# Gate tables by column blocks, early work in another order, and the first one-hots made on GpSimd, in a two-block transformer kernel

## The reference

```python
def block(xb):                                   # 128 tokens
    q = (xb @ w_query).reshape(TOKEN_BLOCK, P_HEADS, 2, P_HALF)
    s = jnp.einsum('thpk,hpnk->thpn', q, sub_keys).astype(jnp.float32)
    sv, si = lax.top_k(s, P_TOPK)                # 16 of 128 keys, twice
    cand = (sv[:, :, 0, :, None] + sv[:, :, 1, None, :]).reshape(TOKEN_BLOCK, P_HEADS, P_TOPK * P_TOPK)
    cidx = (si[:, :, 0, :, None] * N_KEYS + si[:, :, 1, None, :]).reshape(TOKEN_BLOCK, P_HEADS, P_TOPK * P_TOPK)
    fv, fpos = lax.top_k(cand, P_TOPK)
    eidx = jnp.take_along_axis(cidx, fpos, axis=-1)
    g = jax.nn.softmax(fv, axis=-1)
    u = u_tab[eidx]
    act = jax.nn.gelu(jnp.einsum('td,thkd->thk', xb, u).astype(jnp.float32), approximate=False)
    return jnp.einsum('thk,thkd->td', (g * act).astype(xb.dtype), v_tab[eidx])
```

## Time and profile before

| | us |
|---|---|
| median of 3 runs (2775.04 to 2776.07) | 2775.61 |
| the profiled execution | 2776.91 |
| its span | 2775.0 |
| first gate table, last gate table | 1548.7, 1827.7 |
| first dense values, last | 1850.6, 2761 |

### The profile page before, as it was taken

How to read it: one execution, slowest core, us unless ns; L and a number is a source line. 1 busy time by engine, 2 the same in 40 slices (tenths; PEclk the granted TensorE clock), 3 DMA queues, 4 the chain that set the end, 5 groups by cost and what they waited for, 6 DMA issues and landing times.

```text
span 2775.0 us, 24927 instructions
## 1 busy us (share of the span) xinstructions
PE 2532.4 (91%) x8876; PEld 1459.4 (53%) x8876; DVE 1487.6 (54%) x3441; ACT 652.0 (23%) x1559; POOL 314.1 (11%) x287
## 2 busy tenths in 40 slices
PE   6999999999999999998998877668999999989877
PEld 3454555444444444454586665445666666656533
DVE  5444454220033433236456878856777676766675
ACT  2022364010000012224233445421111112111120
POOL 0000000000000000000001001212222222222230
PEclk9999999999999999999999999889999999999989
DMA  9621021112156411110244656779999999999995
GB/s 368 236 92 61 31 71 51 61 61 91 60 227 227 151 61 61 67 55 31 94 172 148 242 187 229 306 265 354 405 387 388 388 389 400 395 400 379 369 370 208
DMA packets 120742, 592.33 MB, mean 213 GB/s; under 512 B 10000, under 2 KB 42768, under 8 KB 76592
## 3 DMA queue, kind: packets, MB, share of 16 engines
q0 software_dynamic: 40656, 321.93, 29.4%
q1 hardware_dynamic: 76944, 247.48, 24.4%
q10 hardware_dynamic: 3024, 21.40, 1.9%
HBM read 571.90 MB, written 18.87 MB: 213 GB/s over the span
## 4 chain that ended last, share of the span: by engine, by line
PE 73%; DMA 14%; DVE 10%; issue 1%; ACT 1%; SPq 1%; POOL 0%; DVEq 0%; ACTq 0%; POOLq 0%
PE PS L609 24%; PE PS L1579 12%; PE PS L1628 11%; DMA arena<-in_u_turned 9%; PE PS L639 8%; PE PS L1151 4%; PE PS L1197 3%; PE PS L794 2%; DMA arena<-in_peer_uv 1%; PE PS L1602 1%; PE PS L814 1%; PE PS L803 1%; DMA arena<-in_ada 1%; DVE arena L2221 1%; PE PS L1172 1%
## 5 line engine op out<-in xcount | busy, mean ns | idle before, releaser
L1579 PE MATMUL PS<-hT,arena 128*128 128x256 f32 x2048 | 488.4, 395 | 60.4 <-DMA arena<-in_u_turned 60.4
L1579 PEld LDWEIGHTS PS<-hT,arena 128*128 128x128 f32 x2048 | 406.5, 199 | 171.6 <-DMA arena<-in_u_turned 71.1
L609 PE MATMUL PS<-arena,ring 128*128 128x512 f32 x832 | 359.2, 593 | 2.1 <-issue 0.8
L609 PE MATMUL PS<-hT,ring 128*128 128x256 f32 (+1 forms) x928 | 303.2, 486 | 7.0 <-ACT arena L1779 4.1
L2342 POOL DMA_INDIRECT arena<-in_peer_uv,arena x151 | 176.2, 1167 | 1158.3 <-DVE arena L2153 465.7
L609 PEld LDWEIGHTS PS<-arena,ring 128*128 128x128 f32 x832 | 157.0, 190 | 203.2 <-issue 201.9
L609 PEld LDWEIGHTS PS<-hT,ring 128*128 128x128 f32 x928 | 179.4, 196 | 124.7 <-issue 103.5
L2182 DVE CUSTOM_DVE_ANT_0 arena<-arena 128x1024 f32<-128x1024 f32 x151 | 183.9, 1222 | 97.5 <-DMA arena<-in_peer_uv,arena 95.5
L639 PE MATMUL PS<-hT,ring 128*128 128x512 f32 x512 | 221.9, 596 | 1.7 <-ACT hT L429 1.7
L1628 PE MATMUL PS<-arena,hT 128*128 128x512 f32 x384 | 173.6, 598 | 14.1 <-DVE hT L2231 14.1
L2199 DVE SCALAR_TENSOR_TENSOR arena<-arena 128x1024 f32<-128x1024 f32 x114 | 146.1, 1281 | 42.8 <-ACT arena L1796 42.5
(11 more groups left out here) (349 smaller groups left out, 2893.6 us busy)
## 6 DMA issues: line engine op xcount, KB each, us to landing
ring<-in_wstream SPq DMA_DIRECT2D x45, 2048.0 KB, 7.9
arena<-in_u_turned SPq DMA_DIRECT2D x128, 512.0 KB, 9.0
arena<-in_peer_uv SPq DMA_DIRECT2D x128, 512.0 KB, 9.2
arena<-in_ada POOLq DMA_DIRECT2D x24, 2048.0 KB, 9.4
gate_tables<-arena ACTq DMA_DIRECT2D x16, 1024.0 KB, 5.8
arena<-gate_tables SPq DMA_DIRECT2D x16, 1024.0 KB, 22.7
arena<-in_peer_uv,arena POOLq DMA_INDIRECT x151, 9.4
xT<-in_xT POOLq DMA_DIRECT2D x1, 2048.0 KB, 18.6
```

The costliest lines, as they stand in the source:

```text
L609: ins = pe.matmul(o, l, r, start=(a == 0), stop=(a == len(lhs) - 1))
L1579: ins = pe.matmul(dense_bank(j), ubuf[j % 3][:, tile(k)], hT[:, k, 256:512], start=(k == 0), stop=(k == KD - 1))
```

## The change

Five things are changed at once.

1. **First one-hots on GpSimd.** They leave VectorE, are made in GpSimd's queue between gathers, and go to six buffers instead of two. An alternative way to make them on ScalarE, not used before, is deleted.
2. **Another row of beats.** 20 beats in place of 24, with one pick in each of the first 12, two in the next four, three in the last four: NEARLY is 32 in place of 56. Jobs of block 3 are mixed in from the third on. All tables lie in beats 12 to 19, eight in each, after the dots of their beat; before, four in each of beats 8 to 23. The dense dots ahead of the loop lie in beats 11 to 19 by the table `DOT_PAIRS`, the last three pairs behind the last tables. Beats 0 to 8 have their values between the queries.
3. **Gate tables in DRAM by column blocks.** The store now writes 512-byte pieces to 16 blocks, and the load of a block is one run of 8 KB for each partition. Before, the store was one run of 8 KB and the load was in 512-byte pieces.
4. **Gates of the dense blocks in one go.** Instead of an exponential, a reciprocal and a product for each head, one exponential over 128 columns for each block, and three VectorE operations (`dense_gates`).
5. **Numbers that follow:** 1.78 picks for a chunk, `turn(xT, 1)` at chunk 80 in place of 70, the first result store at chunk 100 in place of 80.

```diff
-NBEAT = 24
+NAONE = 6
+NBEAT = 20
 def first_pick(b):
-    return 2 * b if b < 16 else 32 + 3 * (b - 16)
+    return b if b < 12 else 12 + 2 * (b - 12) if b < 16 else 20 + 3 * (b - 16)
-GATHER_JOB_AT = {4: 1, 11: 2, 18: 3, 22: 4}
+BEAT_JOB = [(2, 0), (2, 1), (3, 0), (2, 2), (2, 3), (3, 1), (2, 4), (2, 5), (3, 2), (3, 3), (2, 6), (2, 7),
+            (3, 4), (3, 5), (3, 6), (3, 7)]
+GATHER_JOB_AT = {11: 1, 16: 2}
+def values_after(b):
+    return 10 + (5 * b + 1) // 2
+QBEAT = 9
+DOT_PAIRS = {11: 1, 12: 2, 13: 2, 14: 1, 15: 1, 16: 1, 17: 1, 19: 3}
+TABLE_BEAT = 12
+def beat_tables(b):
+    return range(8 * (b - TABLE_BEAT), 8 * (b - TABLE_BEAT) + 8) if b >= TABLE_BEAT else range(0)
 def pick_at(chunk):
-    return NEARLY + (max(0, chunk) * 173) // 100
+    return NEARLY + (max(0, chunk) * 178) // 100
...
             def load_gates(blk):
-                sp.dma_start(gstage[blk % 2].rearrange("p (a c) -> p a c", a=16),
-                             gates_in_dram[:, :, blk * P:(blk + 1) * P].rearrange("a p c -> p a c")).then_inc(g_loaded[blk % 2], 16)
+                sp.dma_start(gstage[blk % 2], gates_in_dram[blk]).then_inc(g_loaded[blk % 2], 16)
...
-            for b in range(6, NBEAT):
-                values(beat_picks(b - 1))
-                if b >= 7:
-                    for q in range(4):
...
-                        if b >= 8:
-                            gate_tables(4 * (b - 8) + q)
+            for b in range(QBEAT, NBEAT):
+                if b > QBEAT:
+                    values(beat_picks(b - 1))
+                if b < NBEAT - 1:
+                    beat_dots(b)
+                if b in (12, 16):
+                    turn_picks(b // 16)
+                for g in beat_tables(b):
+                    gate_tables(g)
+            beat_dots(NBEAT - 1)
             values(beat_picks(NBEAT - 1))
...
                 if g % 4 == 3:
                     act.wait_ge(g_ev, g + 1)
-                    act.dma_start(gates_in_dram[tg], gstage[tg % 2]).then_inc(g_stored[tg % 2], 16)
+                    act.dma_start(gates_in_dram[:, :, tg * P:(tg + 1) * P].rearrange("b p c -> p b c"),
+                                  gstage[tg % 2].rearrange("p (b c) -> p b c", b=16)).then_inc(g_stored[tg % 2], 16)
...
+            def dense_gates(td):
+                q = slice(NGT * PH + PH * td, NGT * PH + PH * td + PH)
+                g = gate[:, 2 + td, :].rearrange("p (h e) -> p h e", h=PH)
+                dve.wait_ge(gates_ex, td + 1)
+                own(dve.tensor_reduce(gsum[:, 0, q], g, AXX, ALU.add))
+                own(dve.reciprocal(gsum[:, 1, q], gsum[:, 0, q]))
+                dve.tensor_tensor(g, g, gsum[:, 1, q].unsqueeze(2).to_broadcast([P, PH, PK]), ALU.mult).then_inc(picks_ok, 1)
...
+            def first_one_hots(g):
+                if g % 32 == 0:
+                    pool.wait_ge(picks_ev, g // 32 + 1)
+                if g >= NAONE:
+                    pool.wait_ge(g_pe, g + 1 - NAONE)
+                pick_i, pick_g = picked[g // 32][0], picked[g // 32][2]
+                for q in range(4):
+                    c = 4 * (g % 32) + q
+                    ins = pool.tensor_scalar(aone[:, g % NAONE, q, :], const("iota"), pick_i[:, c:c + 1], pick_g[:, c:c + 1],
+                                            ALU.is_equal, ALU.mult)
+                ins.then_inc(a_ok, 1)
+
+            made = 0
             for n in range(NPICK):
                 t, e, j = n // NSLOT, n % NSLOT, slot_of(n)
+                while made < 64 and PREVIOUS[n] is not None and PREVIOUS[n] >= first_pick(TABLE_BEAT + made // 8):
+                    first_one_hots(made)
+                    made += 1
```

More of the change, by code:

```diff
@@ L107, in on_pe @@
     return n < NEARLY
-def made_on_dve(g):
-    return True
-MADE_DVE, MADE_ACT = [0], [0]
-for _g in range(64):
-    MADE_DVE.append(MADE_DVE[-1] + made_on_dve(_g))
-    MADE_ACT.append(MADE_ACT[-1] + (not made_on_dve(_g)))
-def dense_pair(b, q):
-    m = 3 * (b - 7) // 2 + q
-    return m + 1 if 7 <= b < 15 and m < 3 * (b - 6) // 2 else 0
 def pick_at(chunk):
-    return NEARLY + (max(0, chunk) * 173) // 100
+    return NEARLY + (max(0, chunk) * 178) // 100
 TURN, PE_BEFORE, DVE_BEFORE = [0] * NPICK, [0] * (NPICK + 1), [0] * (NPICK + 1)
@@ L322, in build @@
         over = cst[:, CCOL["mask"]:CCOL["iota"]]
-        pick_i, pick_j, pick_g, minus_i, minus_g = (over[:, tile(q)] for q in range(5))
-        away = over[:, 5 * P:9 * P].rearrange("p (q n) -> p q n", q=4)
+        picked = [[over[:, tile(3 * td + q)] for q in range(3)] for td in range(2)]
         g2row = sq
@@ L1569, in _ @@
                     ins.then_inc(g2_pe, 1)
-                if i >= 13 and i % 4 == 1:
-                    values(beat_picks((i - 9) // 4 - 1))
+                for b in query_beats(i):
+                    values(beat_picks(b))
             key_scores(15)
@@ L1860, in _ @@
                 if b in GATHER_JOB_AT:
-                    hd = GATHER_JOB_AT[b]
-                    gate_exps(JOB[hd // PH, hd % PH])
-                if b in (8, 16):
-                    copy_picks(b // 8 - 1)
-                if b >= 7:
-                    for q in range(4):
-                        if q < 2 and dense_pair(b, q):
-                            dense_gelu(dense_pair(b, q) - 1)
-                        if b >= 8:
-                            g = 4 * (b - 8) + q
-                            if not made_on_dve(g):
-                                first_one_hots(g)
-                            if g >= 1:
-                                copy_gate_table(g - 1)
-            copy_gate_table(63)
+                    gate_exps(GATHER_JOB_AT[b])
+                if b in (11, 15):
+                    dense_gate_exps(b // 15)
+                if b < NBEAT - 1:
+                    for m in range(DOT_PAIR0[b], DOT_PAIR0[b + 1]):
+                        dense_gelu(m)
+                if b in (12, 16):
+                    copy_picks(b // 16)
+                for g in beat_tables(b):
+                    copy_gate_table(g)
+            for m in range(DOT_PAIR0[NBEAT - 1], DOT_PAIR0[NBEAT]):
+                dense_gelu(m)
             m = AHEAD // 2
@@ L2262, in _ @@
             job(0)
-            gated = 0
             for b in range(NBEAT):
                 if b < 16:
-                    k = JOB[2 + b // 8, b % 8]
-                    job(k, gated)
-                    gated = k
-                picks = beat_picks(b)
-                dot(picks[0])
-                if b in (16, 19, 23):
-                    pick_gates(gated)
-                for n in picks[1:]:
+                    job(JOB[BEAT_JOB[b]])
+                if b == 0:
+                    pick_gates(0)
+                for n in beat_picks(b):
                     dot(n)
@@ L2300, in _ @@
                     hd = (n + back) // PK
-                    if (n + back) % PK == 0 and 5 <= hd < NGT * PH:
-                        piece(JOB[hd // PH, hd % PH])
+                    if (n + back) % PK == 0 and 3 <= hd < NGT * PH:
+                        piece(hd if piece is pick_gates else JOB[hd // PH, hd % PH])
                 if n >= NSLOT and n - NSLOT in LAST_AT:
```

145 lines of the change are left out of this document (55 added, 90 removed).

## The result

The changed kernel takes 2813.64 us (median of 4 runs, 2805.68 to 2818.76), the kernel before 2775.84 on the same chip (2775.04 to 2782.68). The ratio is 1.0128, with a 95% interval of 1.0097 to 1.0159: slower by 38 us, where 2722 was forecast and the range ended at 2800. The profiled execution took 2816.74 us, its span is 2814.7.

What follows compares the result with a forecast made beforehand. It took VectorE's queue to set the time before 1828 us and the DMA engines after 1851, TensorE close behind. Terms 0 - 83 + 5 + 9 + 16 = -53 from the median of 2775.6 gave 2722 us, range 2665 to 2800.

Steps and rivals of the forecast that it cites:

- t: Table stage: time of one 128x128 one-hot on GpSimd, taken as 0.5 us between ends of 0.27 and 0.93.
- rival A: Table stage: slow GpSimd one-hots, by the operation itself or standing still beside VectorE; 2800 at 0.8 us; chance 0.30.
- the formula: Table stage: sum of beats from values, dots, tables, gathers and 32 one-hots each; 196 us against 279, -83.
- Early part, 0: 1373 to 1549 us: VectorE has less to do, but TensorE's order of dots gives it back; 0.
- ScalarE behind the stores in pieces, +5: Table stage: copies and pick weights stand behind gate-table stores in 512 B pieces on ScalarE's queue; +5 us.
- rival D: Table stage: ScalarE stands behind the stores in pieces for 50 us, not 5; about 2767; chance 0.04, no change.
- Between the stages, +9: Last table to first dense values: three pairs of dots and u loads come ahead, 22.9 us becomes 32; +9.
- Dense loop, +16 in all: Dense loop: 24 more gathers cost time, partly given back by spare DMA share, shorter pauses and cheaper gate loads; +16 us.
- -15 for the pieces: Dense loop: 14 gate loads in 8 KB instead of 512 B pieces save between 4 and 25 us; -15 taken.
- +62 - 25 + 4 = +41: Dense loop: 24 added gathers +62, spare DMA share at the end used -25, last token block finished later +4.
- Rival C: Dense loop: held by late loads, not DMA time, added gathers in slack; gains about 50, 2656 us; chance 0.09.
- Rival B: Table stage: one-hots below 0.4 us, TensorE bounds most beats; about 2685 to 2700 us; chance 0.17.

Runs made afterwards that it cites:

- part 3 alone: The kernel before with only the gate tables in DRAM by column blocks (512-byte pieces in stores, 8 KB in loads); 2721.37 us, 0.9811.

## Why the prediction was wrong

**The step that failed is t, the time of a one-hot on GpSimd.** The prediction took 0.5 us, between VectorE's 0.27 and a gather's 0.93, since "128 columns of the same work are nearer to VectorE's row than to a gather". It is 0.782 alone and 0.94 with VectorE's two-input instructions beside it. So rival A came, with both of the causes that it named: the operation alone is 0.782 (72 us above 256 x 0.5), and the overlap with VectorE adds 41, where it was reckoned at 62. The two, 113 us, are as large as the whole difference between the stage forecast (196) and measured (308.5).

That the formula is so near at this t, 305 us at 0.93, is in part luck. It left out TensorE's low clock behind the waits: the values of this stage take 41.8 us where the same values take 30.3 with the one-hots on VectorE, and a beat's last eight table matmuls take 2.08 where eight take 1.05 at the full clock. By these rows that is an estimated 20 us, on the chain. It counted on the other side every gather of a beat, of which the chain shows one, and TensorE's 23 us in beat 13 fell under the longer one-hots.

The time shows the rest: by the prediction's own 26 us for each 0.1, a t of 0.94 gives some 2836. The measured 2813.64 is lower, mostly because the loop gained 3 us where it was to lose 16. The nearest row was chosen by kind of work and not by engine; the gather of 0.93, the one row of GpSimd's queue that was looked at, was the nearer one. Of the -83 forecast, +29.5 came.

The Trainium skill was weighed there. By its "GPSIMD Engine Reference", sections 3.1 and 4.1, I had estimated 0.28 us and a dispatch, with one-input work near line rate. The trace disagrees: 0.78 us at two operations and 0.59 at one, of which some 0.36 to 0.40 is fixed, against 0.27 on VectorE. Its "SBUF — State Buffer", section "Who interferes with whom", says that a VectorE instruction with two SBUF inputs contends with a GpSimd instruction that reads SBUF, and that one with a single input, outside the modes that use both port pairs, does not. The trace agrees on both points: 1.30 us in the mean beside a second one-hot, and 0.783 beside single-input searches.

**Early part, 0.** +5.0 came (1553.7 for 1548.7); in the run with the one-hots on VectorE it is +0.4. Right.

**ScalarE behind the stores in pieces, +5.** With part 3 alone the stage is 279.3 for 279.0. They cost nothing that shows; rival D is out.

**Between the stages, +9.** Measured +8.3, 31.2 us against the forecast 32.

**Dense loop, +16 in all.** Measured -3.1 behind the slower one-hots, and -8 in the run with them on VectorE (916.7 for 924.4). Two sizes in it were off and went against each other. Part 3 alone was worth 57 us in the loop, where the prediction had -15 for the pieces and -10 for the pause behind the late loads; it saw TensorE's 60 us of waits for u and missed VectorE's 111 us of waits for the gate loads, which stood in none of its rows. These waits were no price either: in the run that issued the whole load earlier they went, and the gain was 9 us. The -15 is near the 18 that the packets' durations give; what the term left out is what the pieces do by when and how they are issued, and a part that stays open. The 24 gathers and what comes with them cost +49.5, where +62 - 25 + 4 = +41 was forecast. The -25 was too much: the picks do not just last to the end. The last dense weights stand at pick 32 + 1.78 x 113 = 233, since VectorE makes them 14 chunks ahead, and 23 picks are left then. TensorE is done 47.7 us before the end, at a DMA share of 0.52, so the spare share was moved from in front of TensorE's end to behind it. Making the picks denser did not win it back.

Rival C, a loop held by late loads, was given 0.09. Its gain of about 50 is near the 57 that part 3 alone gave in the loop, but it also wanted the added gathers to lie in slack, and they cost 49.5. Rival B had no footing.

Together: had t been 0.5, the kernel would have come to an estimated 2813.6 - 113 = 2701 us, inside the range, with two terms of the loop wrong by 32 and 8 us. That would have been luck.

## What to carry to other kernels

An instruction moved to another engine has to be priced by a row of that engine, however different its work: the fixed part of GpSimd's one-hot (0.36 to 0.40 us of 0.78 here) is larger than the whole instruction on VectorE (0.27), and VectorE's work with two SBUF inputs beside it added 41 us more. Before a load in small pieces is called cheap, look up every engine that waits for it, not only the one that the page names, and don't take the wait for the price: here VectorE's 111 us of waits were worth 9, since behind them it waited for ScalarE. Of the pieces' harm, by the steps above, 23 of 52 us were how and when they were issued. And when several edits come in one change, undo the doubtful one first: without the one-hots on GpSimd the same change is 0.964 in place of 1.013.

## What the runs showed of the hardware

- **TensorE's clock follows the waits.** In the table stage after, the granted clock is 0.65 in the mean, and on the chain each beat's last eight table matmuls, at the stage's low level, 1.2 GHz, take 2.08 us. Where no wait stands in front, the same eight also appear at 1.05, the 2.4 GHz level of the earlier trace rows. Two rows of TensorE's timeline after:

```profile
1642.81 2.08 PE L1607 MATMUL PS<-arena 128*128 128x128 f32 x8 [1.02 <-POOL arena L2308]
...
1664.69 1.05 PE L1607 MATMUL PS<-arena 128*128 128x128 f32 x8
```

  With the one-hots on VectorE the stage's clock is 0.96. GpSimd's shortest one-hot is 0.78 us also in the run with every fourth one there, at a clock of 0.95. But the last tables of a beat and the values stand on the chain ahead of GpSimd's next gather, so the low clock costs an estimated 20 us of the 308.5 (not tried by itself).
- **The same load lands much later from the other queue.** The load of 2048 pieces lands in 22.7 us on SP's queue and in 40.4 on ScalarE's, while SP's queue carries u and v.
- **One core's DMA engines moved 413 GB/s** over 600 us, with nearly all bytes in 8 KB and 4 KB packets; the kernel before, with 2048 pieces of 512 bytes in every 60 us, drew 390. The Trainium skill's "DMA: Bandwidth & Descriptors", section "Specifications", puts the smallest transfer for line rate at 512 bytes. The trace disagrees: 512 bytes in 30 ns are 17 GB/s of one DMA engine, 8 KB in 317 ns are 26.
